# SSD head loop of a hybrid encoder: masks added to the diagonal blocks alone, two groups' Silu gates made in one visit

## The chip, the cores and the metric

One core of a Trainium2 chip runs the whole program. The metric is device time in microseconds (us). TensorE (PE in the profile) multiplies, VectorE (DVE) and GpSimd (POOL) do elementwise work, ScalarE (ACT) evaluates functions such as Exp and Silu, and SyncE (SP) issues most transfers. The engines run side by side, each through its own list of instructions in order; semaphores are all that ties them together.

## The reference, cut to what matters

Two layers: a gated DeltaNet mixer, then a Mamba-2 SSD mixer, each followed by an expert layer. The change works in the SSD mixer (and touches the making of a mask that the DeltaNet mixer has too). With 256 tokens, 32 heads in 4 groups of 8, and head width 64:

```
seg = exp(where(incl, acum[i] - acum[j], -inf))      # decay between two tokens, incl: lower triangle
cb = einsum('bclgn,bcsgn->bclsg', Cc, Bc)
y_diag = einsum('bclsgr,bcsgrp->bclgrp', cb * seg, X)
...
y = scan forward + flipped scan backward + d_skip * xs
y = y * silu(z)                                      # the gates, group by group
y = rmsnorm over each group's 512 channels
return y @ w_out
```

The kernel takes the 256 tokens as two blocks of 128 and builds, for each head, the whole 256 x 256 matrix of decays: forward on and below the diagonal, backward on and above it.

## The kernel before

Weights come from memory through a ring of units; each unit is used in two halves. ACT rounds a half into its high part (`split_half`, L1555), DVE or POOL makes the low part (L1019, L1958), and PE multiplies with both (`part_mm`, three products).

In the SSD layer a loop of 32 heads runs on four engines at once, each with its order written out by hand:

- PE, in iteration h: `gate_half(h)` (six 512-column products of the gate projection z), `spread(h + 1)`, `y_head(h - 2)`. At h = 8, 16 and 24 `gate_half(h)` stands last, since its banks must first be emptied. `spread` fills three 128-column blocks of a bank for each of the two source blocks: one product lays a row of cumulated decays over all partitions, the second adds `mask`, by a product with the identity. The outer two blocks hold a diagonal block each (forward and backward) and take 0 or -1e30; the middle block is full and gets zeros. `spread(h)` waits until ACT is done with head h - 2, whose banks it takes.
- ACT: four Exps of head h (L1792 to L1795, into `s_E`), then `split_half` of the half that PE uses four heads later, which waits until PE has done `gate_half(h)`. After heads 10, 18 and 26 `group_gate` applies Silu to a finished group of gates (L1775); Silu and Exp stand in different tables, so a table load stands before and after. After heads 14, 22 and 30 `group_squares` sums squares for the norm (L1783).
- POOL: the sum of forward and backward decays of a head (L2037), at h = 1, 9, 17 and 25 the skip term of a group (L2029), and after the sums of heads 12, 20 and 28 the product of a group's y with its gates (L2046, two instructions).
- DVE: the low part of the half (L1019), `weigh(h)` (L1286: decays times cb, into `s_M`), every fourth head `four_out` (L1293), and at h = 7, 15, 23 `gate_out` (L1300), which copies a group's gates out of PE's banks before `weigh`.

`y_head(h)` waits for `weigh(h)`, which waits for POOL's sum, which waits for ACT's Exps. ACT's Exps of head h wait for `weigh(h - 2)`, whose buffer they take. Every list is in order, so whatever stands late on one engine holds all that is behind it.

## Time and profile before

| | us |
|---|---|
| median of 3 runs (2128.32 to 2129.73) | 2129.42 |
| the profiled execution | 2131.4 |
| its span, first to last instruction | 2129.6 |
| PE busy | 2085.3 |
| DVE busy | 1495.8 |
| ACT busy | 1295.5 |
| POOL busy | 1033.8 |

The head loop takes about 100 of these, from 1156 to 1256 us after the span's start. The busy share of an engine says how much it works, not whether it sets the time; which it is at a given place is read from its timeline: the time from one instruction's start to the next one's, against its own duration, and what it waited for.

### The profile page before, as it was taken

How to read it: one execution, taken by the hardware profiler on the slowest of the kernel's cores; microseconds unless marked ns; L12 is line 12 of the kernel's file. 1: busy time of each engine (PE TensorE's matmuls, PEld its weight loads, DVE VectorE, ACT ScalarE, POOL GpSimd, SP SyncE). 2: the span in 40 equal slices, each digit the busy share in tenths (PEclk: the TensorE clock that was granted, in tenths of full speed). 3: DMA queues.
4: the chain of work that ended last, by engine and by line, in shares of the span. 5: the costliest groups of instructions: out<-in, count | busy, mean ns of one | idle time of the engine just before them, and what ended most of it. 6: DMA issues, size and time to landing. Idle time of an engine off the chain costs nothing.

```text
span 2129.6 us, 46196 instructions
## 1 busy us (share of the span) xinstructions
PE 2085.3 (98%) x14416; PEld 1919.6 (90%) x14416; DVE 1495.8 (70%) x3363; ACT 1295.5 (61%) x2621; POOL 1033.8 (49%) x831
## 2 busy tenths in 40 slices
PE   7999899999999999999999999999999999999998
PEld 6989899999999988888899878999999998888886
DVE  4776429947888577777767672499388885777776
ACT  6765555577777544444477775656777774444444
POOL 5751578887777400000067448788877772000000
PEclk9999999999999999999999999999999999999999
DMA  5520355555545566666645235555555556666664
GB/s 167 160 69 21 99 159 171 185 169 165 153 156 157 193 190 194 192 193 195 190 138 160 89 89 188 159 178 177 180 155 150 156 158 188 195 190 195 190 196 148
DMA packets 94162, 343.68 MB, mean 161 GB/s; under 512 B 10720, under 2 KB 10784, under 8 KB 93696
## 3 DMA queue, kind: packets, MB, share of 16 engines
q1 hardware_dynamic: 92880, 338.21, 51.2%
q0 software_dynamic: 912, 4.07, 0.6%
q8 instruction: 48, 0.79, 0.1%
q10 hardware_dynamic: 288, 0.34, 0.1%
q14 instruction: 34, 0.28, 0.0%
HBM read 341.53 MB, written 1.05 MB: 161 GB/s over the span
## 4 chain that ended last, share of the span: by engine, by line
PE 83%; POOL 8%; issue 4%; ACT 2%; DVE 1%; DMA 1%; POOLq 0%; DVEq 0%; SPq 0%; ACTq 0%
PE bank L374 81%; POOL w_lo L1958 8%; DMA ring<-in_gdn_qkv 1%; ACT w_hi L1553 0%; PE bank L554 0%; ACT arena L1553 0%; ACT arena L1580 0%; DVE arena L1117 0%; PE bank L476 0%; PE bank L766 0%; PE bank L636 0%; ACT hT_hi L1553 0%; PE bank L408 0%; DVE arena L1145 0%; PE bank L651 0%
## 5 line engine op out<-in xcount | busy, mean ns | idle before, releaser
L1958 POOL TENSOR_TENSOR w_lo<-ring,w_hi 128x512 fp32r<-128x512 f32 x744 | 948.2, 1298 | 621.5 <-ACT w_hi L1553 612.2
L1553 ACT ACTIVATE w_hi<-ring 128x512 fp32r<-128x512 f32 x1280 | 800.9, 629 | 519.2 <-PE bank L374 510.5
L374 PE MATMUL bank<-hT_hi,w_hi 128*128 128x256 f32 x2688 | 771.7, 287 | 8.7 <-DVE hT_lo L974 4.4
L374 PE MATMUL bank<-hT_hi,w_lo 128*128 128x256 f32 x2688 | 760.6, 283 | 0.0
L374 PE MATMUL bank<-hT_lo,w_hi 128*128 128x256 f32 x2688 | 756.8, 283 | 0.0
L374 PEld LDWEIGHTS bank<-hT_hi,w_hi 128*128 128x128 f32 x2688 | 516.3, 192 | 15.0 <-POOL w_lo L1958 7.3
L1019 DVE TENSOR_TENSOR w_lo<-ring,w_hi 128x512 fp32r<-128x512 f32 x536 | 378.1, 705 | 197.1 <-ACT w_hi L1553 189.6
L374 PEld LDWEIGHTS bank<-hT_hi,w_lo 128*128 128x128 f32 x2688 | 516.4, 192 | 0.0
L374 PEld LDWEIGHTS bank<-hT_lo,w_hi 128*128 128x128 f32 x2688 | 514.7, 192 | 0.1
L374 PE MATMUL bank<-w_hi,p_ag_hi 128*128 128x512 f32 x1024 | 398.4, 389 | 0.0
L374 PE MATMUL bank<-w_lo,p_ag_hi 128*128 128x512 f32 x1024 | 398.4, 389 | 0.0
L374 PE MATMUL bank<-w_hi,p_ag_lo 128*128 128x512 f32 x1024 | 398.3, 389 | 0.0
L374 PEld LDWEIGHTS bank<-w_hi,p_ag_lo 128*128 128x128 f32 x1024 | 192.2, 188 | 40.3
L374 PEld LDWEIGHTS bank<-w_lo,p_ag_hi 128*128 128x128 f32 x1024 | 192.2, 188 | 39.8
L374 PEld LDWEIGHTS bank<-w_hi,p_ag_hi 128*128 128x128 f32 x1024 | 192.2, 188 | 39.6
L1448 DVE SCALAR_TENSOR_TENSOR p_A<-bank,work 128x256 f16<-128x256 f32 x384 | 162.3, 478 | 34.4 <-PE bank L374 23.8
L374 PE MATMUL bank<-arena 128*128 128x128 f32 (+2 forms) x1072 | 133.3, 277 | 7.7 <-ACT arena L1553 3.8
L374 PEld LDWEIGHTS bank<-arena 128*128 128x128 f32 x1072 | 129.4, 193 | 11.3 <-issue 3.0
L1046 DVE SCALAR_TENSOR_TENSOR arena<-bank,small,arena 128x254 f32<-128x254 f32 x192 | 92.4, 482 | 48.7 <-ACT arena L1553 43.4
L1509 DVE TENSOR_TENSOR p_ag_lo<-arena,p_ag_hi 128x256 fp32r<-128x256 f32 x256 | 110.7, 432 | 8.9
L1469 DVE TENSOR_TENSOR arena<-bank,arena 128x256 f32 (+1 forms) x130 | 54.5, 419 | 64.7 <-ACT bank L1865 41.5
L1858 ACT ACTIVATE arena<-bank 128x256 f32 (+1 forms) x112 | 43.0, 384 | 84.2 <-PE bank L374 84.0
(266 smaller groups left out, 2090.5 us busy)
## 6 DMA issues: line engine op xcount, KB each, us to landing
ring<-in_peer_u SPq DMA_DIRECT2D x256, 512.0 KB, 3.5
ring<-in_peer_v SPq DMA_DIRECT2D x256, 512.0 KB, 3.7
ring<-in_peer_wq SPq DMA_DIRECT2D x32, 512.0 KB, 3.5
ring<-in_gdn_qkv SPq DMA_DIRECT2D x24, 512.0 KB, 3.6
ring<-in_ssd_xbc SPq DMA_DIRECT2D x24, 512.0 KB, 3.5
ring<-in_ssd_z SPq DMA_DIRECT2D x16, 512.0 KB, 3.5
ring<-in_ssd_out SPq DMA_DIRECT2D x16, 512.0 KB, 3.5
ring<-in_gdn_z SPq DMA_DIRECT2D x8, 512.0 KB, 3.5
```

The lines of the kernel that those rows point to most:

```text
L374: return pe.matmul(o, w, r, start=first, stop=last)
L1019: dve.tensor_tensor(w_part[1][:, s, :], ring[:, n % RING, hf * 512:(hf + 1) * 512], w_part[0][:, s, :].bitcast(F32), ALU.subtract).then_in ...
L1046: ins = dve.scalar_tensor_tensor(o, bank[:, lo + s:hi + s], taps[:, tile, j:j + 1], o, ALU.mult, ALU.add)
L1448: dve.scalar_tensor_tensor(p_A[:, 4 * (q % 2) + u], lane, p_T[:, 0, tok], p_T[:, 2:4, tok].to_broadcast([P, 2, P]), ALU.is_equal, ALU.mult ...
L1469: dve.tensor_tensor(row, PS[i % 2][:, 0:T], row, ALU.mult).then_inc(SEM["p_gated"], 1)
L1509: dve.tensor_tensor(p_ag[1][:, i % 2, :], v, p_ag[0][:, i % 2, :].bitcast(F32), ALU.subtract).then_inc(SEM["p_ag"], 1)
L1553: return act.activation(o, i, ACT.Copy, scale=scale)
L1858: act.activation(o, PS[i % 2][:, 0:T], ACT.Gelu).then_inc(SEM["p_gelu"], 1)
L1958: pool.tensor_tensor(w_part[1][:, s, :], ring[:, n % RING, hf * 512:(hf + 1) * 512], w_part[0][:, s, :].bitcast(F32), ALU.subtract).then_i ...
```

## The change

- In `spread` the mask product covers the two diagonal blocks alone: 2 x 128 columns in place of 384, read and written with the middle block left out. The zeros of the middle block, and the DVE operation that made them, go; the waits on the mask's semaphore count 3 and 6 in place of 4 and 8. The DeltaNet layer's masks were never read from the middle block.
- ACT: the gates of group 0 are no longer made after head 10 but after head 18, together with those of group 1, behind one table load. Those of group 2 stay after head 26.
- ACT: the squares of group 0 move from after head 14 to after head 22, ahead of those of group 1.
- POOL: the products with the gates move from after the sums of heads 12 and 20 to after those of heads 19 and 21. That of group 2 stays after head 28.

```diff
@@ PE, spread
-                        last = mm(o, mask[:, 3 * P:4 * P], mask[:, 0:3 * P], False, True)
+                        diagonal, masks = (v.rearrange("p (b i) -> p b i", b=3)[:, 0:3:2, :] for v in (o, mask[:, 0:3 * P]))
+                        last = mm(diagonal, mask[:, 3 * P:4 * P], masks, False, True)
@@ DVE, make_mask
-                dve.tensor_scalar(mask[:, P:2 * P], upper, 0.0, None, ALU.mult).then_inc(SEM["masked"], 1)
@@ ACT, head loop
-                    if h > SR and h % SR == 2:
-                        group_gate(h // SR - 1)
-                    if h > SR and h % SR == 6:
+                    if h == 2 * SR + 2:
+                        group_gate(0)
+                        group_gate(1)
+                    if h == 3 * SR + 2:
+                        group_gate(2)
+                    if h > 2 * SR and h % SR == 6:
+                        if h < 3 * SR:
+                            group_squares(0)
                         group_squares(h // SR - 1)
@@ POOL, head loop
-                if h > SR and h % SR == 4:
-                    g = h // SR - 1
+                if h in (2 * SR + 3, 2 * SR + 5, 3 * SR + 4):
+                    g = {2 * SR + 3: 0, 2 * SR + 5: 1, 3 * SR + 4: 2}[h]
                     pool.wait_ge(SEM["s_y"], 2 * (g + 1))
```

On POOL, from head 9's sum to head 24's, before (L2037 the sums, L2029 the skip term, L2046 the products with the gates):

```order
L2029 TENSOR_TENSOR arena<-arena,small 128x512 x2
L2037 TENSOR_TENSOR arena<-arena 128x2x128 x3
L2046 TENSOR_TENSOR arena<-arena 128x512 x2
L2037 TENSOR_TENSOR arena<-arena 128x2x128 x5
L2029 TENSOR_TENSOR arena<-arena,small 128x512 x2
L2037 TENSOR_TENSOR arena<-arena 128x2x128 x3
L2046 TENSOR_TENSOR arena<-arena 128x512 x2
```

and now (the same operations are L2042, L2034 and L2051, the file being five lines longer there):

```order
L2034 TENSOR_TENSOR arena<-arena,small 128x512 x2
L2042 TENSOR_TENSOR arena<-arena 128x2x128 x8
L2034 TENSOR_TENSOR arena<-arena,small 128x512 x2
L2042 TENSOR_TENSOR arena<-arena 128x2x128 x2
L2051 TENSOR_TENSOR arena<-arena 128x512 x2
L2042 TENSOR_TENSOR arena<-arena 128x2x128 x2
L2051 TENSOR_TENSOR arena<-arena 128x512 x2
```

The first pair of products has moved eight heads back, and the two pairs now stand with two sums between them.

On ACT, around the gates after head 18, before (L1553 is the split, L1792 and L1795 the first and last Exp of a head):

```order
L1795 ACTIVATE arena<-bank,small 128x256
L1553 ACTIVATE w_hi<-ring 128x512
L1775 ACT_TABLE_LOAD
L1775 ACTIVATE arena<-arena 128x512 x2
L1792 ACT_TABLE_LOAD
L1792 ACTIVATE arena<-bank,small 128x256
```

and now:

```order
L1795 ACTIVATE arena<-bank,small 128x256
L1553 ACTIVATE w_hi<-ring 128x512
L1775 ACT_TABLE_LOAD
L1775 ACTIVATE arena<-arena 128x512 x4
L1792 ACT_TABLE_LOAD
L1792 ACTIVATE arena<-bank,small 128x256
```

Two more Silus stand between head 18's split and head 19's Exps; after head 10 the split is now followed by head 11's Exps directly.

On PE, one `spread`, before:

```order
L374 MATMUL bank<-p_ag_hi,pick 128x384
L374 MATMUL bank<-p_ag_lo 128x384
L374 MATMUL bank<-p_ag_hi,pick 128x384
L374 MATMUL bank<-p_ag_lo 128x384
L374 MATMUL bank<-w_hi,hT_hi 128x512
```

and now:

```order
L374 MATMUL bank<-p_ag_hi,pick 128x384
L374 MATMUL bank<-p_ag_lo 128x2x128
L374 MATMUL bank<-p_ag_hi,pick 128x384
L374 MATMUL bank<-p_ag_lo 128x2x128
L374 MATMUL bank<-w_hi,hT_hi 128x512
```

The order of PE's instructions is the same; the two mask products of each head have lost the middle block.

## Rows read from the trace of the kernel before

**Rows 1.** The page, part 1: busy us, share of the span, instructions.
```profile
PE 2085.3 (98%) x14416; PEld 1919.6 (90%) x14416; DVE 1495.8 (70%) x3363; ACT 1295.5 (61%) x2621; POOL 1033.8 (49%) x831
```

**Rows 2.** Windows, all engines: stretch and its length, busy us, clock, DMA.
```profile
1120.00:1130.00 10.00, 10.00 (x84) 9.89 (x83) 8.60 (x19) 7.27 (x17) 7.73 (x7) 1.00 0.57 167
...
1158.00:1253.00 95.00, 94.31 (x563) 84.61 (x562) 65.91 (x79) 77.00 (x187) 48.51 (x47) 1.00 0.32 101
```

**Rows 3.** Timeline of PE: start, duration, operation. 256 columns; end of `spread(18)`, `y_head(16)`; `gate_half(18)` and `(19)`.
```profile
1154.87 0.28 PE L374 MATMUL bank<-hT_hi,w_lo 128*128 128x256 f32 x1
1154.99 0.28 PE L374 MATMUL bank<-hT_hi,w_hi 128*128 128x256 f32 x1
...
1209.29 0.34 PE L374 MATMUL bank<-p_ag_lo 128*128 128x384 f32 x1
1209.47 1.00 PE L374 MATMUL bank<-arena 128*128 128x64 f32 x8
1210.28 0.47 PE L374 MATMUL bank<-w_hi,hT_hi 128*128 128x512 f32 x1
...
1213.25 0.48 PE L374 MATMUL bank<-w_hi,hT_hi 128*128 128x512 f32 x1
```

**Rows 4.** Timeline of PE: the end of `gate_half(20)`, `spread(21)`; `y_head(22)`, `gate_half(24)`.
```profile
1217.48 0.40 PE L374 MATMUL bank<-w_hi,hT_lo 128*128 128x512 f32 x1
1217.82 0.44 PE L374 MATMUL bank<-p_ag_hi,pick 128*128 128x384 f32 x1
...
1229.17 1.00 PE L374 MATMUL bank<-arena 128*128 128x64 f32 x8
1230.21 0.50 PE L374 MATMUL bank<-w_hi,hT_hi 128*128 128x512 f32 x1
```

**Rows 5.** Timeline of ACT after head 18, then after head 22.
```profile
1212.01 0.63 ACT L1553 ACTIVATE w_hi<-ring 128x512 fp32r<-128x512 f32 x1 [0.70 <-PE bank L374]
1212.65 1.28 ACT L1775 ACT_TABLE_LOAD   x1
1213.95 1.15 ACT L1775 ACTIVATE arena<-arena 128x512 f32<-128x512 f32 x2
...
1216.42 0.48 ACT L1792 ACTIVATE arena<-bank,small 128x256 f32<-128x256 f32 x1
...
1224.69 0.61 ACT L1783 ACTIVATE arena<-arena 128x512 f32<-128x512 f32 x1
...
1226.25 0.48 ACT L1792 ACTIVATE arena<-bank,small 128x256 f32<-128x256 f32 x1
```

**Rows 6.** Timeline of POOL: sum of head 19, products of group 1, sums 21 and 22.
```profile
1217.85 0.74 POOL L2037 TENSOR_TENSOR arena<-arena 128x256 f32<-128x256 f32 x1 [3.45 <-ACT arena L1795]
...
1220.30 3.45 POOL L2046 TENSOR_TENSOR arena<-arena 128x512 f32<-128x512 f32 x2
1223.72 1.86 POOL L2037 TENSOR_TENSOR arena<-arena 128x256 f32<-128x256 f32 x2
```

**Rows 7.** Timeline of DVE: `weigh(20)`, `weigh(21)`, low part 23, `gate_out(2)`.
```profile
1220.82 1.78 DVE L1286 TENSOR_TENSOR arena<-arena 128x512 f32<-128x512 f32 x1
...
1224.93 1.20 DVE L1286 TENSOR_TENSOR arena<-arena 128x512 f32<-128x512 f32 x1 [0.63 <-POOL arena L2037]
...
1228.15 0.80 DVE L1019 TENSOR_TENSOR w_lo<-ring,w_hi 128x512 fp32r<-128x512 f32 x1 [0.21 <-ACT w_hi L1553]
1228.88 1.27 DVE L1300 COPY arena<-bank 128x512 f32<-128x512 f32 x2
```

**Rows 8.** Timeline of PE: two places with long idle time before an instruction.
```profile
126.54 1.14 PE L374 MATMUL bank<-arena 128*128 128x128 f32 x8 [2.63 <-ACT arena L1553]
...
1255.34 1.10 PE L374 MATMUL bank<-arena 128*128 128x64 f32 x8 [2.23 <-DVE arena L1286]
```

**Rows 9.** Windows, the two stretches at a lower clock that follow them.
```profile
1257.30:1264.00 6.70, 5.10 (x16) 4.06 (x16) 5.30 (x10) 4.72 (x10) 0.00 (x0) 0.50 0.04 15
...
127.20:131.00 3.80, 3.80 (x18) 3.41 (x17) 2.51 (x9) 1.37 (x5) 0.76 (x1) 0.55 0.77 258
```

More of the change, by code:

```diff
@@ L530, in gdn @@
                     if h == 0:
-                        pe.wait_ge(SEM["masked"], 4)
+                        pe.wait_ge(SEM["masked"], 3)
                     spread_row(PS[h % 2], h).then_inc(SEM["g_bc"], 1)
@@ L702, in ssd @@
                 pe.wait_ge(SEM["s_cumsb"], 1)
-                pe.wait_ge(SEM["masked"], 8)
+                pe.wait_ge(SEM["masked"], 6)
                 def spread(h):
```

## The prediction, made before the changed kernel had run

> **What bounds the kernel now.** I read the page first. PE is busy in 98% of the span [rows 1], so an edit counts where it shortens PE's own stream or makes PE wait. Then the windows over the head loop: PE busy in 94.31 of 95.00 us, ACT in 77.00, DVE in 65.91, POOL in 48.51 [rows 2]. PE is the bound there, but ACT is four fifths full, and an engine that full covers for a lump of work only if its list has room at that place. So I read the timelines of all four engines through one group of heads. What to see in them: PE runs head after head in 2.97 us (gate_half(18) begins at 1210.28, gate_half(19) at 1213.25 [rows 3]), and slips only where ACT's gates hold it up.
>
> That slip is the measure of everything below. ACT's split after head 18 starts at 1212.01, as soon as PE is done with gate_half(18); I call this moment zero. Then come the table load (0.64), two Silus (1.94 to 3.09), the load back, and head 19's Exps (4.41) [rows 5]. PE's spread(21) needs these Exps done and starts at 1217.82, or 5.81. PE was at its last product of gate_half(20) at 1217.48, and products of 512 columns follow each other by 0.23 here (six and the step to the next piece take 1.48), so it could have gone on at 1217.71: it waits 0.11 [rows 4]. So ACT is already exactly as late as PE can bear. gate_half(24) starts at 1230.21, or 18.20 [rows 4].
>
> **The mask products.** A 384-column product holds PE 0.18 us (1209.29 to 1209.47), a 256-column one 0.12 (1154.87 to 1154.99) [rows 3]. The starts are rounded; at the granted clock of 1.00 [rows 2], which is 2.4 GHz, 128 columns are 0.053, and I take 0.054 for each of 64: 0.107 a head, 3.4 in all; a head takes 2.87. The trace has no 2 x 128 product with a gap in it. Its bounds: the 256-column row (0.12) and, if the gap costs as much as the columns saved, the 384-column row (0.18), so a gain of 3.4 or nothing; I take 0.12, since it has those very columns. The removed DVE operation stands ahead of the loop, in a stretch where PE is busy 10.00 of 10.00 us [rows 2]; PE's work hides it, and without that cover it would give back its own length once. I put it at nothing.
>
> Of the 3.4 us little arrives. Between two visits to the Silu table, ACT, POOL and DVE run a chain that hangs on one moment of PE (the end of gate_half(10), (18) or (26)) and not on PE's pace, and PE meets it again at spread(13), (21), (29) and at gate_half(16), (24). Where PE comes earlier, it waits longer. Five spreads lie between spread(13) and gate_half(16), two between the anchor and spread(13): 7 x 0.107 = 0.75 of a group's 0.86 is handed back. By itself I put this edit at -1.2: 0.1 in each of three groups, plus the first heads, which have no gates behind them.
>
> **The gates of group 0 leave head 10.** ACT is rid of two loads and two Silus there, 1216.42 - 1212.65 = 3.77 us in the twin of head 18 [rows 5]; POOL of 3.44 after head 12 (1220.30 to 1223.72 [rows 6]), ACT of 1.56 after head 14 (1224.69 to 1226.25 [rows 5]). In heads 8 to 16 nothing then waits: PE gains its wait of 0.11 at spread(13) and one of 0.23 at gate_half(16). This one is read off its twin, gate_half(24): a y_head holds PE 0.81 (1209.47 to 1210.28 [rows 3]), but from y_head(22) to gate_half(24) it is 1.04 [rows 4]. With 16 spreads (3 to 18) at 0.107, moment zero of group 2 comes 1.7 + 0.3 = 2.05 us earlier.
>
> **They come back after head 18.** Times from zero:
> ACT does two more Silus, 1.15 [rows 5]: head 19's Exps start at 5.56, end at 6.91, spread(21) starts at 6.96. PE, two shortened spreads quicker, is there at 5.70 - 0.21 = 5.49. It waits 1.47 where it waited 0.11.
> POOL sums head 19 at 5.84 + 1.15 = 6.99 [rows 6], then at once multiplies group 0, 7.7 to 11.1. Until now a further sum stood ahead of the products. While POOL multiplies, DVE stands: weigh(20), begun 0.5 us after the products, took 1.78 us where such an operation takes 0.7, and ended as POOL's first product had ended plus 0.57; weigh(21) came 4.63 after the products' start [rows 6, 7]. Laid one head forward: weigh(19) ends at 10.0, POOL's sum(20) runs 11.1 to 12.3, weigh(20) ends at 13.5.
> Head 21's Exps need weigh(19): 10.1 to 11.4. sum(21) ends at 13.0, and the products of group 1 follow at once, to 16.5. They hold weigh(21) until 16.5 + 0.57 = 17.1.
> Head 22's Exps need weigh(20): 13.6 to 15.0; split to 15.5; squares of group 0 to 17.0, of group 1 to 18.5 (1.56 a pair before, read-outs included [rows 5]); head 23's Exps to 19.9.
> PE meanwhile: spread(22) at 9.85, spread(23) at 12.7; y_head(20) waits some 0.25, y_head(21) 0.6 (reached 16.45, needs weigh(21)); it reaches spread(25) at 17.9, which needs head 23's Exps, and waits 2.0, to 19.9. Before, this place had no wait.
> DVE: low part of half 27 at 20.4 (after ACT's split), then gate_out(2), 0.73 + 1.2 us later [rows 7], done at 22.4. gate_half(24) is reached at 21.4 and waits 1.1, to 22.5, where it stood at 18.20: 4.3 us later.
> Here stands a rule of the Trainium skill, SBUF — State Buffer, section "SBUF: two separate sides": DVE operations with two SBUF inputs and GpSimd's operations share a port pair that is held for a whole instruction, and the loser blocks. The trace agrees (1.78 us for a 0.7 us operation), and by it the two pairs of products so near each other speak against this change. Without it, weigh(21) would end about 1 us earlier, and the sum would change little, since the squares end at 18.5 either way.
>
> **The sum.** -2.05 before zero, +4.3 to gate_half(24), -0.1 after it (spreads 26 to 31 give 0.64, the meeting points at spread(29) and at the last y_heads take 0.5 back). That is **+2.1, taken as +1.9** because the steps were rounded up. Against the profiled execution (2131.4, of which the span is 2129.6) it gives 2133.3; the median of the runs is 2129.42, so I predict **2131.3**. The expert stage behind the loop is PE's own stream and passes a shift on as it is. The gates' edit alone I put at +3.9 (PE then has the full 2.97 a head and loses only what ACT's list costs), the mask's alone at -1.2. A measurement of this kernel can tell 0.2%, 4.3 us, from no change, so this counts as the same.
>
> **Rivals.**
> *The clock falls.* The waits at y_head(21), spread(25) and gate_half(24) are 0.6, 2.0 and 1.1 us inside some 6. The granted clock of the loop is 1.00 [rows 2], and fell to 0.5 (1.2 GHz) after idle times of 2.63 us, and of 2.23 with another behind it [rows 8], for 3.8 and 6.7 us [rows 9]. For: nearly the same idle share. Against: never one wait that long, and real work between. Price: half of that time, 1.9 to 3.4 us, on top of 1.9: 3.8 to 5.3, so 2133.2 to 2134.7, **slower** by over 0.2% where it reaches 4.3. It decides if the wait at spread(25) comes near 2.2.
> *The gain goes through.* If the list of ACT has more room than I count (squares or products overlap better), the waits of group 2 shrink to under a microsecond and PE keeps 1 to 3.4 of its shortened products: 2126.0 to 2128.9. Against: the 0.11 us of slack in rows 4 is measured.
> *Fewer table loads are worth their time.* 2 x 1.28 us off ACT [rows 5]; if ACT, not PE, set the loop, the end would come 2.6 earlier, with all of the mask's 3.4 some 6: 2123.4, **faster**. Against: ACT is idle 18 of 95 us [rows 2]. The Trainium skill, ScalarE: Activation LUTs, section "Table sets: the hidden batching unit", says just this, batch calls by table set; and its section "What ACT_TABLE_LOAD costs" adds a drain of about 1.38 us to each load. Here the next operation starts 0.02 us after the load, so the trace doesn't agree with the drain; by the page's figure the estimate of ACT's saving would be 5.3 in place of 2.6.
> *The mask product isn't cheaper.* Then the gates' edit stands alone: +3.9, 2133.3.
>
> **How the numbers follow.** Forecast 0.60 (own range 2129.8 to 2132.8, from rounding some ten steps); clock falls 0.16, half of it above 4.3; gain goes through 0.14; table loads 0.03; mask not cheaper 0.07, a third of it over the bound. Faster 0.03; slower 0.08 + 0.02 + 0.02 for mixtures = 0.12; same 0.85. The range leaves out the far ends of both sides: 2127.2 to 2134.2.
>
> **What would show it.** In the profile after: mask products of 0.12 us apart; no Silu table load after head 10; no wait of PE from spread(3) to gate_half(18); then a wait of about 1.5 before spread(21) on ACT's Exps, of 2 before spread(25), of 1 before gate_half(24) on gate_out; weigh(19) and weigh(21) at about 1.8 us; gate_half(24) 22.5 us after the split that follows gate_half(18), and the granted clock at 1.00 up to the last y_head. It would be wrong if spread(25) waits under 1 us, if the clock falls within the loop, or if the products stay 0.17 to 0.18 apart.

## The result, and the profile after

The changed kernel takes **2132.24 us** (median of 22 runs, 2129.60 to 2134.28), the kernel before 2129.48 beside it (22 runs, 2127.11 to 2131.89). The ratio is 1.0013, with a 95% interval of 1.0007 to 1.0018: 2.8 us slower, less than the 0.2% that the prediction calls no change. The prediction was 2131.3 in a range of 2127.2 to 2134.2.

The page of the kernel after, part 1, answers to [rows 1] (two instructions fewer on ACT, two on DVE):

```profile
PE 2084.6 (98%) x14416; PEld 1917.0 (90%) x14416; DVE 1497.1 (70%) x3361; ACT 1292.4 (61%) x2619; POOL 1033.6 (49%) x831
```

Read like this, nothing has happened: PE has 0.7 us less to do, and the kernel is longer. The mask product of 2 x 128 columns stands here as 256 and holds PE 0.12 us, where the one of 384 held it 0.18 [rows 3]:

```profile
1209.18 0.28 PE L374 MATMUL bank<-p_ag_lo 128*128 128x256 f32 x1
1209.30 0.34 PE L374 MATMUL bank<-p_ag_hi,pick 128*128 128x384 f32 x1
```

The new waits lie behind head 18, and the longest has a second effect. Here is PE at `spread(21)`, then from `y_head(21)` to the third product of `gate_half(24)` (start, duration, operation, and in brackets the idle time before it with what ended it); the twin of the last lines is in [rows 4]:

```profile
1213.25 0.44 PE L374 MATMUL bank<-p_ag_hi,pick 128*128 128x384 f32 x1 [1.22 <-ACT arena L1795]
...
1223.22 1.10 PE L374 MATMUL bank<-arena 128*128 128x64 f32 x8 [0.19 <-DVE arena L1286]
1226.07 0.44 PE L374 MATMUL bank<-p_ag_hi,pick 128*128 128x384 f32 x1 [1.74 <-ACT arena L1795]
...
1228.62 0.80 PE L374 MATMUL bank<-w_hi,hT_hi 128*128 128x512 f32 x1
...
1229.65 0.63 PE L374 MATMUL bank<-w_hi,hT_lo 128*128 128x512 f32 x1
1230.07 0.63 PE L374 MATMUL bank<-w_hi,hT_hi 128*128 128x512 f32 x1
```

`spread(25)` waits for head 23's Exps: `y_head(21)` has given its last product by 1224.03 (it holds PE 0.81), so PE stands 2.04 us. (The bracket counts from the modelled end of the product before and says 1.74. I call the first number a wait and the second an idle time; idle times are 0.15 to 0.3 shorter.) And behind that wait the 512-column products come 0.42 to 0.43 apart, not 0.23. The windows say why (stretch and its length, busy us of PE, PEld, DVE, ACT and POOL, granted clock, DMA share, GB/s):

```profile
1223.00:1226.07 3.07, 1.14 (x10) 0.97 (x9) 2.50 (x4) 2.97 (x11) 0.75 (x1) 1.00 0.41 165
1226.30:1233.10 6.80, 6.80 (x23) 5.84 (x23) 3.39 (x6) 2.92 (x10) 1.25 (x2) 0.51 0.24 77
```

PE was busy 1.14 of 3.07 us, and then the granted clock was 0.51 (1.2 of 2.4 GHz) for 6.8 us. Before, the clock was 1.00 from 1158 to 1253 [rows 2].

ACT after head 18 and after head 22, to be held against [rows 5]:

```profile
1206.40 0.63 ACT L1553 ACTIVATE w_hi<-ring 128x512 fp32r<-128x512 f32 x1 [0.61 <-PE bank L374]
1207.05 1.28 ACT L1775 ACT_TABLE_LOAD   x1
1208.34 2.19 ACT L1775 ACTIVATE arena<-arena 128x512 f32<-128x512 f32 x4
1210.55 1.28 ACT L1792 ACT_TABLE_LOAD   x1
1211.85 0.47 ACT L1792 ACTIVATE arena<-bank,small 128x256 f32<-128x256 f32 x1
...
1221.63 0.64 ACT L1783 ACTIVATE arena<-arena 128x512 f32<-128x512 f32 x1
...
1224.66 0.47 ACT L1792 ACTIVATE arena<-bank,small 128x256 f32<-128x256 f32 x1
```

Moment zero is 1206.40. One visit to the table holds all four Silus, and head 19's Exps begin 5.45 after zero. Both pairs of squares stand between 1221.63 and 1224.66, and nothing is idle between them: `spread(25)` waits for what stands behind them.

POOL's two pairs of products and DVE beside them, to be held against [rows 6, 7]:

```profile
1213.96 3.43 POOL L2051 TENSOR_TENSOR arena<-arena 128x512 f32<-128x512 f32 x2
...
1219.20 3.42 POOL L2051 TENSOR_TENSOR arena<-arena 128x512 f32<-128x512 f32 x2
```

```profile
1214.48 1.77 DVE L1286 TENSOR_TENSOR arena<-arena 128x512 f32<-128x512 f32 x1
...
1221.38 1.78 DVE L1286 TENSOR_TENSOR arena<-arena 128x512 f32<-128x512 f32 x1
```

`weigh(19)` and `weigh(21)` take 1.77 and 1.78 us, as the prediction has it.

**Stages.** To find the other differences I cut each profile at lines of PE that occur in every kernel. The view of one source line gives the first and last start of its products; first the kernel before (a second profile of it, the run `before_again` below), then the kernel after:

```profile
L651 PE MATMUL bank<-const,arena x32: 270/272/274, 1111.6 to 1156.2; 128*128 128x128 f32 x32
L766 PE MATMUL bank<-const,arena x32: 270/272/477, 1255.0 to 1289.1; 128*128 128x128 f32 x32
```

```profile
L651 PE MATMUL bank<-const,arena x32: 270/272/300, 1111.5 to 1155.9; 128*128 128x128 f32 x32
L767 PE MATMUL bank<-const,arena x32: 270/272/477, 1258.5 to 1294.2; 128*128 128x128 f32 x32
```

L651 is `turn_tok`, L766 and L767 are `turn_y`. A third mark, L408, turns the residual ahead of each expert stage. So the head loop (last product of `turn_tok` to first of `turn_y`) takes 1255.0 - 1156.2 = 98.8 us before and 102.6 after. All profiles, cut in the same way; the last four columns are us of each kernel's profile, from the span's start to the first L408, of the head loop, from the first product of `turn_y` to the last L408, and from there to the end:

| kernel | median us (runs) | against before | to first L408 | head loop | to last L408 | to the end |
|---|---|---|---|---|---|---|
| before, both profiles | 2129.48 (22) | 1 | 258.3, 255.1 | 98.8, 98.8 | 54.2, 53.9 | 817.3, 817.4 |
| after, both profiles | 2132.24 (22) | 1.0013 (1.0007 to 1.0018) | 255.0, 255.2 | 102.6, 102.6 | 55.5, 55.3 | 816.4, 816.3 |
| mask_only | 2127.40 (11) | 0.9990 (0.9981 to 0.9999) | 256.8 | 97.8 | 54.6 | 816.3 |
| mask_keep_zero | 2127.67 (11) | 0.9993 (0.9984 to 1.0002) | 255.0 | 97.8 | 54.3 | 817.6 |
| gates_only | 2136.05 (6) | 1.0030 (1.0018 to 1.0042) | 255.5 | 105.3 | 54.2 | 817.4 |
| after_warm | 2132.37 (11) | 1.0013 (1.0004 to 1.0022) | 254.9 | 102.9 | 55.1 | 816.6 |
| after_wide_fill | 2130.71 (11) | 1.0000 (0.9990 to 1.0009) | 256.5 | 100.5 | 54.8 | 816.3 |
| after_squares_apart | 2130.03 (11) | 0.9997 (0.9988 to 1.0006) | 256.7 | 99.2 | 55.4 | 816.4 |
| after_small_products | 2129.53 (11) | 0.9998 (0.9989 to 1.0008) | 256.4 | 101.6 | 54.2 | 816.6 |
| mask_gates_early | 2125.74 (11) | 0.9981 (0.9972 to 0.9990) | 256.4 | 95.6 | 55.3 | 816.4 |
| mask_gates_early_late_products | 2123.71 (7) | 0.9973 (0.9961 to 0.9984) | 254.7 | 94.6 | 54.2 | 816.6 |
| late_products_gate_out_first | 2122.96 (5) | 0.9965 (0.9952 to 0.9979) | 256.6 | 93.4 | 55.0 | 816.4 |

What is left out between the first L408 and the loop is the same everywhere (856.4 or 856.5 to the first L651, then 44.4 to 44.6). The loop and the last column repeat within 0.1 between two profiles of one kernel, and I argue from them.

The other two columns follow the granted clock. The start differs by up to 3.6 us, and by 3.2 between the two profiles of the kernel before. In the six profiles where the clock is 1.00 near 20 us it takes 254.7 to 255.2; in seven a stretch at 0.50, 3.4 to 3.5 us long, lies there and it takes 255.5 to 256.8; in the first profile of the kernel before that stretch is 6.8 long and it takes 258.3. Around `turn_y` the clock is low in every profile, for 6.8 to 6.9 us in four and 10.2 to 10.3 in ten, and the column "to last L408" is 51.0 plus half of what of this stretch lies behind the first product of `turn_y`, within 0.2 in all fourteen. So spans of single profiles don't compare.

### The profile page after: what moved, and what is told of

It reads as the page before. It is cut to its first block, busy times and chain, and to the rows that moved or that the text cites. A ratio compares the mean times of both kernels' runs of the same rounds, so it can differ in the third digit from the quotient of the medians.

```text
span 2130.4 us, 46193 instructions
## 1 busy us (share of the span) xinstructions
PE 2084.6 (98%) x14416; PEld 1917.0 (90%) x14416; DVE 1497.1 (70%) x3361; ACT 1292.4 (61%) x2619; POOL 1033.6 (49%) x831
## 4 chain that ended last, share of the span: by engine, by line
PE 82%; POOL 9%; issue 5%; ACT 2%; DVE 1%; DMA 1%; POOLq 0%; DVEq 0%; ACTq 0%
PE bank L374 81%; POOL w_lo L1963 8%; ACT w_hi L1553 1%; DMA small<-in_ssd_d 0%; PE bank L554 0%; ACT arena L1553 0%; DVE arena L1117 0%; PE bank L476 0%; ACT arena L1580 0%; PE bank L767 0%; POOL small L1956 0%; PE bank L636 0%; DMA ring<-in_norm_final 0%; POOL arena L2051 0%; PE bank L408 0%
## 5 line engine op out<-in xcount | busy, mean ns | idle before, releaser
L1553 ACT ACTIVATE w_hi<-ring 128x512 fp32r<-128x512 f32 x1280 | 800.1, 629 | 523.1 <-PE bank L374 514.9
L1448 DVE SCALAR_TENSOR_TENSOR p_A<-bank,work 128x256 f16<-128x256 f32 x384 | 162.4, 478 | 33.2 <-PE bank L374 22.5
L374 PEld LDWEIGHTS bank<-arena 128*128 128x128 f32 x1072 | 128.8, 194 | 12.3 <-issue 3.4
L1469 DVE TENSOR_TENSOR arena<-bank,arena 128x256 f32 (+1 forms) x130 | 54.6, 420 | 64.7 <-ACT bank L1870 40.8
```

The source lines that it names most:

```text
L374: return pe.matmul(o, w, r, start=first, stop=last)
L1448: dve.scalar_tensor_tensor(p_A[:, 4 * (q % 2) + u], lane, p_T[:, 0, tok], p_T[:, 2:4, tok].to_broadcast([P, 2, P]), ALU.is_equal, ALU.mult ...
L1469: dve.tensor_tensor(row, PS[i % 2][:, 0:T], row, ALU.mult).then_inc(SEM["p_gated"], 1)
L1553: return act.activation(o, i, ACT.Copy, scale=scale)
```

## Experiments

The kernels were timed in four groups, each beside the kernel before: mask_only, gates_only, after_warm and mask_gates_early beside a median of 2130.08; after_wide_fill, after_squares_apart, after_small_products and mask_gates_early_late_products beside 2130.10; late_products_gate_out_first and the two repeated profiles beside 2129.93; mask_keep_zero beside 2130.16.

### The halves of the change: mask_only and gates_only

mask_only:

```diff
-                        last = mm(o, mask[:, 3 * P:4 * P], mask[:, 0:3 * P], False, True)
+                        diagonal, masks = (v.rearrange("p (b i) -> p b i", b=3)[:, 0:3:2, :] for v in (o, mask[:, 0:3 * P]))
+                        last = mm(diagonal, mask[:, 3 * P:4 * P], masks, False, True)
...
-                dve.tensor_scalar(mask[:, P:2 * P], upper, 0.0, None, ALU.mult).then_inc(SEM["masked"], 1)
```

> The kernel before with the mask products alone shortened to the two diagonal blocks. My theory (ACT, POOL and DVE hang on the end of gate_half(10), (18), (26) and hand most of PE's gain back): 1.2 us faster than before (0.5 to 1.9), mask products 0.12 us apart, PE waits of about 0.3 before spread(13), (21), (29) and 0.7 before gate_half(16), (24), granted clock 1.00 up to the last y_head. Rival (PE sets the loop everywhere): 3.4 us faster and no longer waits. Rival (the gap costs as much as the columns save): no change.

> The changed kernel with the full 384-column mask products put back: the moved gates, squares and products alone. My theory: 3.9 us slower than before from waits (about 1.2 before spread(21), 2 before spread(25), 1 before gate_half(24)), and in executions in which the granted clock falls behind them another 1.9 to 3.3, so a median between +3.5 and +6.5 us. Rival (two table loads fewer are worth their time): 0 to 2.6 us faster.

gates_only is the rest of the diff, with the mask of before. In mask_only the waits on the mask's semaphore count 3 and 6, as in the change. Measured: mask_only 2127.4, its loop 97.8, 1.0 shorter than before, where 1.2 was expected. But the whole is 2.1 to 2.7 us faster, and its last column is 1.0 shorter too. I take that up again at the end. PE in mask_only, at `spread(21)` and `gate_half(24)`:

```profile
1215.28 0.44 PE L374 MATMUL bank<-p_ag_hi,pick 128*128 128x384 f32 x1 [0.19 <-ACT arena L1795]
...
1227.66 0.50 PE L374 MATMUL bank<-w_hi,hT_hi 128*128 128x512 f32 x1 [0.61 <-DVE arena L1300]
```

The idle times are what the products gave up: `spread(21)` and `gate_half(24)` meet the chain that hangs on moment zero, as expected. gates_only takes 6.0 us more than before, in the upper half of the expected 3.5 to 6.5; its loop is 6.5 longer. Its idle times are 0.98 at `spread(21)`, 1.73 at `spread(25)`, and then:

```profile
1231.04 0.80 PE L374 MATMUL bank<-w_hi,hT_hi 128*128 128x512 f32 x1 [0.77 <-DVE arena L1300]
```

with a window that begins inside this wait:

```profile
1230.40:1237.20 6.80, 6.16 (x15) 5.01 (x16) 2.48 (x4) 2.50 (x6) 1.77 (x3) 0.50 0.27 77
```

So the clock falls here as well, one wait later than in the kernel after, and for the same 6.8 us. Half of these, 3.4, less some of the wait that they hide, on top of the 3.9 expected of the waits, is the 6.5 measured, within a us.

### What the fall of the clock costs: after_warm and after_wide_fill

```diff
+                    if h == 3 * SR:
+                        for e in range(20):
+                            mm(PS[5][:, 3 * SP_:4 * SP_], mask[:, 3 * P:4 * P], mask[:, 0:SP_])
                     if h + 1 < SH:
                         spread(h + 1)
```

> The changed kernel with 20 small products (64 columns, into columns that y_head(23) overwrites) on PE ahead of the wait of spread(25). If the lower clock after that wait is part of the measured +2.8 us: the granted clock stays at 1.00 from spread(25) to the last y_head, gate_half(24) waits about 1 us for gate_out again, and the time is 1 to 2.2 us above before. If the clock adds nothing (or falls for another reason): +2.8 us as the changed kernel, or more by what the 20 products delay.

This missed. The products stood where the wait had been, and the clock fell all the same. They also took 0.5 us too long: `spread(25)` starts 3.35 behind `y_head(21)`, where it was 2.85. So this run doesn't show the price of the fall:

```profile
1223.08 1.10 PE L374 MATMUL bank<-arena 128*128 128x64 f32 x8 [0.18 <-DVE arena L1289]
1223.99 2.62 PE L374 MATMUL bank<-p_ag_lo 128*128 128x64 f32 x20
1226.43 0.67 PE L374 MATMUL bank<-p_ag_hi,pick 128*128 128x384 f32 x1
```

```profile
1222.00:1225.90 3.90, 3.72 (x32) 3.41 (x30) 3.36 (x4) 3.77 (x13) 1.61 (x2) 1.00 0.43 134
1226.10:1232.90 6.80, 6.80 (x24) 6.03 (x24) 2.63 (x5) 2.22 (x7) 1.31 (x2) 0.50 0.28 77
```

PE counts as busy 3.72 of the 3.90 us ahead of the fall. But 20 products of 64 columns took 2.44, 0.12 each, the time in which [rows 3] pass 256. So the second attempt had 16 products of 256 columns at the same place, at the same 0.12 each:

```diff
+                    if h == 3 * SR:
+                        o = PS[5][:, :].rearrange("p (t w) -> p t w", t=NT)[:, :, 2 * SP_:4 * SP_]
+                        m = mask[:, 0:3 * P].rearrange("p (b i) -> p b i", b=3)[:, 0:3:2, :]
+                        for e in range(16):
+                            mm(o, mask[:, 3 * P:4 * P], m)
```

> The kernel after, with 16 products of 256 columns put ahead of spread(25), where PE waits 2.04 us for head 23's Exps; they write columns that y_head(22) and y_head(23) write anew. At 0.12 us each they take 1.9 us, so the wait is filled to within 0.1 and nothing is made later. The earlier filler, 20 products of 64 columns at the same 0.12, left the clock to fall at the same moment as in the kernel after. Theory that the fall comes from this wait and that only products that feed columns at full pace count: the granted clock stays at 1.00 between 1226 and 1233, gate_half(24) waits about 1 us for gate_out again, and since the low stretch of 6.8 us costs half of itself less the 1.0 of wait that it hides, the kernel is 2 to 2.4 us faster than the one after: about 2130. Rival that the fall is set by the whole chain of waits around (0.34 at y_head(21), 1.1 at gate_half(24)) or by a tick that no filler moves: the clock is low again from 1226, and the time is that of the kernel after, 2132.2, within 0.5.

Measured: moment zero (ACT's split), PE from the filler to `gate_half(24)`, and the windows of that stretch and of the loop:

```profile
1207.92 0.63 ACT L1558 ACTIVATE w_hi<-ring 128x512 fp32r<-128x512 f32 x1 [0.61 <-PE bank L374]
...
1225.65 2.15 PE L374 MATMUL bank<-p_ag_lo 128*128 128x256 f32 x16
1227.64 0.39 PE L374 MATMUL bank<-p_ag_hi,pick 128*128 128x384 f32 x1
...
1230.15 0.50 PE L374 MATMUL bank<-w_hi,hT_hi 128*128 128x512 f32 x1 [0.88 <-DVE arena L1305]
```

```profile
1227.50:1234.50 7.00, 6.12 (x40) 5.49 (x39) 4.07 (x7) 4.39 (x13) 2.10 (x3) 1.00 0.21 75
1157.40:1251.40 94.00, 90.82 (x565) 81.13 (x563) 64.73 (x77) 71.97 (x183) 47.80 (x46) 1.00 0.31 100
```

The clock stays at 1.00 up to the last `y_head`, `gate_half(24)` waits for `gate_out` as the prediction had it, and the loop takes 100.5 us where the kernel after takes 102.6. That **2.1 us is the price of the clock's fall** in the loop. `spread(25)` starts 19.72 after zero, as good as in the kernel after (19.67), so nothing but the clock differs there. The time is 2130.71, 1.5 below the kernel after and 0.7 above what was expected. Each filler has one profile; that the width of the products made the difference between them is the likely reading, not a proven one. This also shows the loop as the prediction saw it, with all waits and no fall: 100.5 - 98.8 = **+1.7, where +1.9 was predicted**.

### Why spread(25) waits: after_squares_apart and after_small_products

```diff
-                    if h > 2 * SR and h % SR == 6:
-                        if h < 3 * SR:
-                            group_squares(0)
-                        group_squares(h // SR - 1)
+                    if h in (2 * SR + 6, 2 * SR + 7, 3 * SR + 6):
+                        group_squares({2 * SR + 6: 0, 2 * SR + 7: 1, 3 * SR + 6: 2}[h])
```

> The kernel after, with the squares of group 1 moved from behind head 22 to behind head 23; those of group 0 stay. Theory of the prediction, that spread(25) waits because both pairs of squares (1.5 us each) stand between head 22's and head 23's Exps: head 23's Exps begin 1.4 us earlier, the wait at spread(25) falls from 2.04 to 0.6, gate_half(24) waits 1.3, the moment zero to gate_half(24) takes 1.1 less than the 22.5 forecast, and with a clock that stays at 1.00 the head loop is some 1.1 shorter by the waits and 2 more by the clock: 100 us or less from the first turn_tok's end to turn_y where the kernel after takes 102.6, and 2129.5 to 2131 in all. Rival, that products and weigh set this place and not ACT's list: spread(25) waits over 1.5 us still and the time stays at 2132.2.

The expected thing happened. ACT's split at moment zero, its Exps of head 23 and PE's `spread(25)` and `gate_half(24)`:

```profile
1208.15 0.63 ACT L1553 ACTIVATE w_hi<-ring 128x512 fp32r<-128x512 f32 x1 [0.61 <-PE bank L374]
...
1225.03 0.47 ACT L1792 ACTIVATE arena<-bank,small 128x256 f32<-128x256 f32 x1 [0.16 <-DVE arena L1286]
```

```profile
1226.44 0.44 PE L374 MATMUL bank<-p_ag_hi,pick 128*128 128x384 f32 x1 [0.36 <-ACT arena L1795]
...
1229.11 0.50 PE L374 MATMUL bank<-w_hi,hT_hi 128*128 128x512 f32 x1 [0.97 <-DVE arena L1300]
```

Head 23's Exps begin 16.88 after zero instead of 18.26, 1.4 earlier, and now wait for `weigh(21)`; the idle time before `spread(25)` is 0.36 instead of 1.74, the clock stays at 1.00, and the loop is down to 99.2. Moving two squares behind one head's Exps gives back 3.4 us of the loop: 2.1 of them are the clock's, and 1.3 are waits (100.5 with the clock held up and the squares in place). The median is 2130.03.

after_small_products leaves POOL's products of groups 0 and 1 in place, with 8 columns each instead of 512. It leaves out the gating of the other columns, so only its time is of use:

```diff
-                        v = s_y[:, t, g * 512:(g + 1) * 512]
-                        pool.tensor_tensor(v, v, s_siluz[:, t, g * 512:(g + 1) * 512], ALU.mult).then_inc(SEM["s_yg"], 1)
+                        v = s_y[:, t, g * 512:(g + 1) * 512] if g == 2 else s_y[:, t, g * 512:g * 512 + 8]
+                        z = s_siluz[:, t, g * 512:(g + 1) * 512] if g == 2 else s_siluz[:, t, g * 512:g * 512 + 8]
+                        pool.tensor_tensor(v, v, z, ALU.mult).then_inc(SEM["s_yg"], 1)
```

> The kernel after, with POOL's products of the gates of groups 0 and 1 over 8 columns of 512 only, so the gating of these two groups is left out but for those columns; everything else is as it was. Theory of the prediction: POOL's 3.43 us lumps hold DVE's weigh(19) and weigh(21) to 1.78 us where 0.7 would do, and these make y_head(20) and y_head(21) wait (0.26 and 0.34) and Exps(21), Exps(22) start late, but the squares of both groups still stand ahead of Exps(23). So weigh at 0.6 to 0.7, no wait at y_head(20) and (21), 1.35 at spread(21) as before, 0.9 at spread(25), 1.1 at gate_half(24): 1.6 us less by waits, and if the clock then doesn't fall, 2 more: 2128.5 to 2130.6. Rival, that the products cost nothing since ACT's list alone decides: spread(25) waits 2.0 still, and the time is 2132.

DVE's `weigh(19)` and `weigh(21)`, which have two inputs in SBUF; then ACT's split at moment zero and PE's two waits:

```profile
1215.92 0.69 DVE L1286 TENSOR_TENSOR arena<-arena 128x512 f32<-128x512 f32 x1
...
1219.58 0.69 DVE L1286 TENSOR_TENSOR arena<-arena 128x512 f32<-128x512 f32 x1
```

```profile
1207.84 0.63 ACT L1553 ACTIVATE w_hi<-ring 128x512 fp32r<-128x512 f32 x1 [0.61 <-PE bank L374]
...
1225.73 0.44 PE L374 MATMUL bank<-p_ag_hi,pick 128*128 128x384 f32 x1 [0.76 <-ACT arena L1795]
1228.29 0.80 PE L374 MATMUL bank<-w_hi,hT_hi 128*128 128x512 f32 x1 [0.86 <-DVE arena L1300]
```

`weigh` falls from 1.78 to 0.69 us, so the long ones come from POOL's products. (The Trainium skill, SBUF — State Buffer, section "Who interferes with whom", says that a DVE operation with two SBUF inputs contends with a GpSimd operation that reads SBUF. This pair of runs agrees.) The waits of 0.26 and 0.34 at the two `y_head`s are gone, and the idle time at `spread(25)` is 0.76 instead of 1.74. It is 1.0 shorter, not gone, since the squares still stand there. But PE also gets there sooner: from zero, `spread(25)` starts at 17.89 and `gate_half(24)` at 20.45, each 1.8 earlier than in after_wide_fill (19.72 and 22.23). That is more than the 1.3 us that the squares are worth at `gate_half(24)` (20.96 in after_squares_apart). So of the waits in the chain behind head 18 the larger part comes from POOL's products. How much of it is their hold on DVE and how much POOL's own time for them, this run can't tell, since it takes away both.

Against what I expected, the clock fell all the same, at 1227.7, inside the wait at `gate_half(24)`, for 6.8 us. From `gate_half(24)` to `turn_y` it then takes 30.6 us, where it takes 27.8 in after_wide_fill, and so the loop gave back only 1.0 (101.6). The median, 2129.53, lies in the expected range all the same, but that doesn't bear the forecast out: the profiled execution took 2131.52 and the eleven lie between 2128.04 and 2133.36, so the fall may be missing in some of them, which one profile can't show.

### Versions that beat both: mask_gates_early and two more

If the trouble is ACT's list right behind head 18, the gates can go back to their old heads, and one step earlier: ahead of that head's split, where ACT would be waiting for PE. The diff is against mask_only.

```diff
-                    split_half(at[("sz", 0, 0)] + h // 2 + 2, h % 2)
                     if h > SR and h % SR == 2:
                         group_gate(h // SR - 1)
+                    split_half(at[("sz", 0, 0)] + h // 2 + 2, h % 2)
```

> The kernel before with the short mask products, the gates in their old heads 10, 18 and 26, but ahead of that head's split in place of behind it, so that ACT doesn't wait for gate_half before the table load. My theory (the chain from the end of gate_half(10) through ACT to head 11's Exps hands PE's gain back) gives 2.9 us faster than before (2 to 3.5), that is 1.7 more than the short masks alone, with waits before spread(13), (21), (29) gone. If that chain isn't what hands the gain back: as the short masks alone.

```profile
1207.76 1.28 ACT L1775 ACT_TABLE_LOAD   x1
...
1210.12 0.62 ACT L1553 ACTIVATE w_hi<-ring 128x512 fp32r<-128x512 f32 x1
1210.75 1.28 ACT L1792 ACT_TABLE_LOAD   x1
```

The load to Silu now starts while PE is still in `gate_half(18)`, in the 0.70 us for which ACT waited in [rows 5]. The waits at the three `spread`s are gone, two of 0.35 at `gate_half(16)` and (24) are left, and one of 2.31 at the last `y_head`. The loop is 95.6, 3.2 below before: nearly the whole 3.4 us of the narrower products arrives. In all 2125.74, 3.7 to 4.3 us faster than before (2129.48 and 2130.08); 2 to 3.5 was expected, without the 1.0 us behind the loop that the last experiment finds.

The next one moves POOL's products to the sums of heads 13, 21, 29 and ACT's squares to heads 15, 23, 31:

```diff
-                    if h > SR and h % SR == 6:
+                    if h > SR and h % SR == 7:
                         group_squares(h // SR - 1)
...
-                if h > SR and h % SR == 4:
+                if h > SR and h % SR == 5:
```

> The mask over the diagonal blocks, the gates of each group at their old heads (10, 18, 26) but ahead of that head's split, and now POOL's products one head later (after 13, 21, 29) and ACT's squares one head later (after 15, 23, 31). Theory: with the products a head later weigh of head 30 and 31 are no longer held at the loop's end, so the wait at the last y_head falls from 2.31 to about 1; gate_half(16) and (24) wait 0.4 to 0.5 as before. Expected about 1 us less than with the gates early alone: 2124.8. Rival: the squares behind head 31 now come after the last Exps and delay the means and roots that turn_y waits for, so what y_head(31) gives is taken back there: 2125.7 to 2126.7.

The idle time at the last `y_head` fell from 2.31 to 0.70, those at `gate_half(16)` and (24) rose to 0.46 and 0.47, and the loop is down to 94.6. The median is 2123.71, where 2124.8 was expected. The last version sets `gate_out(h // SR)` ahead of `gate_rest(h)` on DVE:

> The kernel with early gates and late products, and on DVE gate_out ahead of the low part of the same head (7, 15, 23) in place of behind it. There gate_half(24) waits 0.46 us for gate_out, which starts at 1223.02 behind weigh(22), four_out (0.60) and the low part of half 23 (0.60), though PE's gate_half(23) was over at 1221.03. Theory: gate_out starts 0.6 earlier, the waits at gate_half(16) and gate_half(24) (0.46 each) go, and weigh(23) starts no later since both orders end together: head loop 0.9 shorter, 93.7 us, 2122.8 in all. Rival: the low part comes 1.2 later and holds up a later gate_half, or the ended wait comes back at the next Exps: 2123.7 as without it.

Both waits at `gate_half` are gone, the loop is 93.4 (93.7 was expected), and the median **2122.96, 0.35% below the kernel before** (0.21 to 0.48%) and 9 us below the kernel after.

### How far stage times can be trusted: before_again and after_again

> The kernel before, unchanged, for a second profile of it. The head loop (end of turn_tok to turn_y) took 98.8 us in the first; if the differences of stage times by which the other kernels are read mean anything, it is 98.8 again within 0.3, with waits of 0.1 to 0.2 us at spread(13), (21), (29) and a clock of 1.00 in the loop. What lies before turn_raw and behind turn_y may differ by one to three microseconds: there the clock falls at idle times of PE.

> The kernel after, unchanged, for a second profile. If the fall of the clock behind the wait at spread(25) belongs to the kernel, it is there again and the head loop takes 102.6 us as in the first; if it hangs on the moment, the loop takes 100.5 as with the wait filled by wide products.

The loop took 98.8 and 102.6 again. In after_again, PE once more:

```profile
1226.27 0.68 PE L374 MATMUL bank<-p_ag_hi,pick 128*128 128x384 f32 x1 [1.75 <-ACT arena L1795]
```

with the products behind it at the slow pace from the start. So the fall belongs to the kernel and not to the moment; it is in both profiles. (Whether it is in all 22 executions isn't shown: the two fastest took 2129.60 and 2129.72.) The start of before was 255.1, not 258.3, with the clock at 1.00 near 20 us.

### The 1.0 us behind the loop: mask_keep_zero

The last column of the table falls in two: 817.3 to 817.4 for before and gates_only, 816.3 to 816.6 for all others. What these others lack is one DVE operation, the zero block of the mask. It runs twice, once in each layer's mask, 0.22 us each time, at 69.8 and 1118.6 us in mask_keep_zero. So I put it back, and nothing reads it:

```diff
-                        last = mm(o, mask[:, 3 * P:4 * P], mask[:, 0:3 * P], False, True)
+                        diagonal, masks = (v.rearrange("p (b i) -> p b i", b=3)[:, 0:3:2, :] for v in (o, mask[:, 0:3 * P]))
+                        last = mm(diagonal, mask[:, 3 * P:4 * P], masks, False, True)
```

> The mask product over the two diagonal blocks alone, as in mask_only, but DVE still makes the zero block (one operation more in DVE's program, and the semaphore counts of before), which nothing reads now. Every kernel without that operation took 816.3 to 816.6 us from turn_raw of the last layer to the end, every kernel with it 817.3 to 817.4, though it stands long before and this stretch has the same instructions. Theory, that the missing operation itself brings that 1.0 us (through the place of the loops behind it in the program): the last stretch takes 817.4 again, the head loop 97.8 as in mask_only, and the time is 1.0 above mask_only's 2127.4, 2128.4 to 2129. Rival, that the narrower products bring it or that it is chance: 816.3 again and 2127.4. Second rival: the prediction's price of nothing for the operation where it stands is wrong, and the stretch with turn_tok and the norms before it is longer by 0.4 to 0.7 than in mask_only.

The stage is 817.6, as long as with the operation before, and the loop 97.8 as in mask_only; the stretch with `turn_tok` stays at 44.4. The median was to be 2128.4 to 2129 and is 2127.67, 0.3 above mask_only's 2127.40: two medians from two comparisons can't tell 1 us. But the profile shows where it is: in the expert stage's loop of 32 turns, whose 16 fp16 products mark each turn. First with the operation (mask_keep_zero), then without it (mask_only): the fp16 products, the next product, and the fp16 products of the next turn.

```profile
1568.90 1.07 PE L374 MATMUL bank<-p_A,work 128*128 128x128 f16 x16
1569.83 0.38 PE L374 MATMUL bank<-hT_hi,w_hi 128*128 128x256 f32 x1
...
1575.68 1.07 PE L374 MATMUL bank<-p_A,work 128*128 128x128 f16 x16
```

```profile
1570.94 1.07 PE L374 MATMUL bank<-p_A,work 128*128 128x128 f16 x16
1571.82 0.36 PE L374 MATMUL bank<-hT_hi,w_hi 128*128 128x256 f32 x1
...
1577.65 1.07 PE L374 MATMUL bank<-p_A,work 128*128 128x128 f16 x16
```

The step is 6.78 with it and 6.71 without, the next one 6.95 and 6.93; the time is lost where the fp16 products end (0.93 against 0.88, and 0.07 by the second product behind them), and the rest of the turn is the same on PE. All 31 steps of the loop sum to 211.63 and 210.62; to 211.68 in before_again and 211.71 in gates_only, to 210.61 in after_again. The clock is no rival: it is 1.00 from 1320 to 2110 in both. DVE's wait for PE in this stretch is 12.3 us with the operation and 11.0 without.

So it is shown that this operation, dead as it is, costs 1.0 us in a loop that runs 400 us later and has the same instructions in both. That it acts through the place of the loop in DVE's program is only argued: nothing else differs behind it. Against it speaks that the first layer's expert stage, behind the operation at 69.8, shows nothing: from the first L408 to `turn_tok` it is 856.4 or 856.5 us with and without it. The Trainium skill, Runtime: NRT & Kernel Launch, section "Instruction fetch mechanics", says that instructions are fetched in blocks and that a taken branch whose target lies outside the blocks at hand stalls; a loop that lies otherwise across the blocks would fit, but no view here shows the fetch.

## Why the prediction was right, and where it was not

**The mask products** came out as predicted: 0.12 apart where the row of before had 0.18 [rows 3], and mask_only's loop is 1.0 shorter where the term was 1.2. The rival by which they would be no cheaper is out.

**Up to moment zero** the term was -2.05. From `turn_tok`'s last product it is 1212.01 - 1159.3 = 52.7 before and 1206.40 - 1155.9 = 50.5 after: -2.2.

**From zero to gate_half(24)** the term was 22.5 - 18.20 = +4.3; it is 22.22, +4.0, and 22.23 with the clock held up. By its steps: head 19's Exps at 5.45 (5.56 predicted), `spread(21)` at 6.85 (6.96), `spread(25)` at 19.67 (19.9) with a wait of 2.04 (2.0), `gate_half(24)` at 22.2. The wait at `y_head(20)` was sized right (0.26, predicted 0.25); that at `y_head(21)` was 0.34 and not 0.6. PE was there at 16.48, as predicted (16.45), but `weigh(21)` ended at 16.76 and not at 17.1, since the products of group 1 ran from 12.80 to 16.22 and not from 13.0 to 16.5. It costs nothing in the sum, since ACT's list decides at `spread(25)`. after_squares_apart shows that cause: without the two pairs of squares side by side head 23's Exps begin 1.4 earlier. The step that says that the end of DVE's hold "would change the sum little" is not borne out: in after_small_products, which takes away POOL's time for the products as well as the hold, the squares themselves start 1.75 earlier from zero (13.48 against 15.23), and `gate_half(24)` 1.8 earlier. They end 16.5 after zero there and not "at 18.5 either way"; only the clock's fall kept this small in the total.

**The wait at gate_half(24)** is not to be seen in the kernel after. The slow clock stretched `y_head(22)` to 1.6 us and covered it. With the clock held up it is there, 1.07 us where 1.1 was predicted (0.88 of idle time in the profile), and ends at 1230.15 - 1207.92 = 22.23 from zero, the same moment.

**After gate_half(24)** the term was -0.1. With the clock held up it is (1257.9 - 1230.15) - (1258.1 - 1230.21) = -0.1. In the kernel after it is +2.0.

**The failed step is the clock.** The forecast had it at 1.00 up to the last `y_head`; the rival "the clock falls" had 0.16. It did fall, in the place that the rival named, at a wait of 2.04 where it put the point near 2.2 (after [rows 8]), for 6.8 us [rows 9] and at a price of 2.1, inside its 1.9 to 3.4. What I held against it, "real work between", was no protection here: the work between is a `y_head` of 64-column products, and twenty 64-column products in a row did not hold the clock in after_warm. I should have weighed 0.16 higher by far: a wait of 2.0 between other waits is nearer to the 2.23 "with another behind it" than to anything that left the clock alone. In the mechanism the rival was right and my forecast wrong, though its time, 2133.2 to 2134.7, was above the measured one.

**Why the number held anyway.** That was luck in part. Two differences are the same in both profiles of before and after: +3.8 in the head loop, of which 1.7 are waits and 2.1 the clock, and -1.0 in the expert loop. They add up to +2.8, which is the difference of the medians. So 2131.3 came close since a missing +2.1 met a missing -1.0. The two profiles after and before_again differ by more, +1.6 between the loop and the last L408 and -0.3 ahead of the loop: 4.1, and the spans are 2130.4 and 2126.3. The 1.6 is the clock again: behind the first product of `turn_y` it stays low for 8.9 us (to 1267.4), in before_again for 5.6 (to 1260.6), and half of the 3.3 between them is 1.65. Other kernels lie anywhere between 54.2 and 55.4 there. Whether the longer stretch belongs to the kernel after, and how often before has its longer start (258.3 or 255.1), two profiles each don't show.

**The removed DVE operation** was put at nothing. That was right where it stands, and wrong behind it: it gives 1.0 us in a loop that I had not looked at.

**Fewer table loads** gave nothing, as the prediction said, and more: the kernels with early gates keep all six loads in the loop and are 6.5 to 9.3 us faster than the kernel after. It is the place of the visit that counts on ACT here, not the number. **The gain goes through** was the wrong rival for this change (its upper end should read 2128.4, 2129.42 - 1). In mask_gates_early its outcome comes true: with each group's gates ahead of the split PE keeps 3.2 of its 3.4 us.

## What to carry to other kernels

Before batching lumps of work (table visits, squares, products) on an engine that is not the bound but is four fifths full, add up the lumps that land between two operations on which the bounding engine waits: two small lumps in idle places are free, the same two side by side are a wait. Where such waits of one or two microseconds come on TensorE, price the clock's fall with them (2.1 us here, behind one of 2.04); a filler of 256-column products held the clock up here, one of 64-column products did not. And compare stages with the same instructions between two profiles, not spans: that is how a 1 us effect of one removed instruction, and a start that differs by 3 us with the clock, become visible.

## What the runs showed of the hardware that I had not expected

- Twenty 64-column products, back to back at 0.12 us, did not keep the clock from falling; with sixteen 256-column products at the same 0.12 us and in the same place it stayed at 1.00 (one profile each).
- The clock fell with an idle time of 0.76 at `spread(25)` and 0.86 at `gate_half(24)` (after_small_products), and not with 0.36 and 0.97 at the same places (after_squares_apart). The longest wait alone doesn't decide; what does is open.
- In all five profiles with a fall inside the loop (after twice, gates_only, after_warm, after_small_products) the low stretch lasted 6.8 us, whatever PE did in it (busy 6.80 us of it in after and after_warm, 6.16 in gates_only, 6.21 in after_small_products).
- One DVE operation that nothing reads (twice 0.22 us) made a later loop of 32 turns 1.0 us longer, by 0.01 to 0.07 us a turn from the fifth on.
